# Two-layer streaming encoder on one core: the attention's value products taken per head in two passes

## What is computed

```python
def sb_attend(q, k, v, q_pos, k_pos):
    z = jnp.einsum('bqhd,bkhd->bhqk', q, k).astype(jnp.float32) * SB_SCALE
    visible = k_pos[None, :] < q_pos[:, None]
    log_1mb = jnp.where(visible, jax.nn.log_sigmoid(-z), 0.0)
    suffix = lax.cumsum(log_1mb, axis=3, reverse=True) - log_1mb
    a = jnp.where(visible, jnp.exp(jax.nn.log_sigmoid(z) + suffix), 0.0)
    return jnp.einsum('bhqk,bkhd->bqhd', a.astype(v.dtype), v)
```

## Time and profile before

| | us |
|---|---|
| median of three runs | 1851.74 |
| lowest and highest | 1851.21, 1851.76 |
| the profiled execution's own time | 1851.8 |
| its span in the profile | 1850.0 |
| PE busy in that span | 1829.1 |
| mean granted clock | 1.00 |

### The profile page before, as it was taken

One profiled execution on the slowest core, in us unless ns is written; L12 is line 12 of the kernel. 1 busy time (PEld: TensorE's weight loads), 2 busy tenths in 40 slices (PEclk: granted clock), 3 DMA queues, 4 the chain that ended last, 5 costly groups with the idle time before them and its releaser, 6 DMA issues.

```text
span 1850.0 us, 33796 instructions
## 1 busy us (share of the span) xinstructions
PE 1829.1 (99%) x14262; PEld 1773.7 (96%) x14262; DVE 927.8 (50%) x1634; ACT 559.8 (30%) x1197; POOL 1074.3 (58%) x996
## 2 busy tenths in 40 slices
PE   9999999999999999999999999999999999999999
PEld 8999989999999999999999999899999999999999
DVE  6676775232755532523556767752346555235143
ACT  4444443112422211202344444430133222112021
POOL 8685534746555555556666854446456555555564
PEclk9999999999999999999999999999999999999999
DMA  5242112233223222223343421212422222222222
GB/s 188 88 136 73 63 41 81 92 118 115 70 91 92 83 89 92 86 80 97 98 143 93 127 86 47 69 62 88 152 80 75 86 92 89 84 92 92 80 83 95
DMA packets 76231, 170.49 MB, mean 92 GB/s; under 512 B 6384, under 2 KB 34160, under 8 KB 76080
## 3 DMA queue, kind: packets, MB, share of 16 engines
q1 hardware_dynamic: 68752, 160.79, 27.2%
q10 hardware_dynamic: 7328, 7.54, 1.2%
HBM read 156.41 MB, written 9.79 MB: 90 GB/s over the span
## 4 chain that ended last, share of the span: by engine, by line
PE 92%; DVE 5%; ACT 1%; issue 0%; POOL 0%; DMA 0%; SPq 0%; DVEq 0%; ACTq 0%; POOLq 0%
PE ps L1563 76%; PE ps L1598 2%; PE ps L1726 2%; PE ps L1684 2%; DVE xT L1430 1%; DVE xn L1091 1%; DVE mix L1427 1%; PE ps L1775 1%; PE ps L1781 1%; PE ps L1637 1%; PE ps L1703 1%; DVE R L1091 1%; DVE xT L1248 1%; PE ps L1652 1%; PE ps L1749 1%; PE ps L1722 1%
## 5 line engine op out<-in xcount | busy, mean ns | idle before, releaser
L1563 PE MATMUL ps<-xn,wsp 128*128 128x272 f32 x7824 | 1002.4, 289 | 4.2 <-issue 2.2
L1563 PEld LDWEIGHTS ps<-xn,wsp 128*128 128x128 f32 x7824 | 985.4, 189 | 8.2 <-issue 4.1
L612 POOL CAST wsp<-raw 128x1024 fp32r<-128x1024 f32 (+2 forms) x222 | 219.0, 991 | 505.9 <-DMA raw<-in_wstream 452.1
L619 POOL TENSOR_TENSOR wsp<-raw,wsp 128x1024 fp32r<-128x1024 f32 (+2 forms) x278 | 492.3, 1782 | 16.2
L1563 PE MATMUL ps<-R,wsp 128*128 128x272 f32 x3840 | 486.2, 288 | 0.1
L1563 PEld LDWEIGHTS ps<-R,wsp 128*128 128x128 f32 x3840 | 482.7, 189 | 1.2 <-DVE xT L1120 0.5
L606 POOL TENSOR_TENSOR wsp<-raw,wsp 128x256 fp32r<-128x256 f32 x304 | 240.3, 811 | 12.2
L601 POOL CAST wsp<-raw 128x512 fp32r<-128x512 f32 x152 | 106.3, 699 | 151.8 <-DMA raw<-in_wstream 116.1
L1091 DVE SCALAR_TENSOR_TENSOR R<-ps,R 64x256 fp32r<-64x256 f32 (+11 forms) x264 | 129.8, 510 | 72.2 <-ACT R L749 24.9
L1446 DVE TENSOR_TENSOR mix<-ps,rstd 128x272 f32<-128x272 f32 x88 | 38.8, 441 | 202.5 <-PE ps L1563 192.2
L976 ACT ACTIVATE mix<-vv 128x2 f32<-128x2 f32 x88 | 18.0, 204 | 363.0 <-DVE mix L1448 363.0
(11 more groups left out here) (230 smaller groups left out, 1543.0 us busy)
## 6 DMA issues: line engine op xcount, KB each, us to landing
raw<-in_wstream SPq DMA_DIRECT2D x233, 512.0 KB, 3.5
raw<-in_wstream SPq DMA_DIRECT2D x48, 128.0 KB, 2.7
raw<-in_wstream SPq DMA_DIRECT2D x16, 384.0 KB, 3.1
raw<-in_kc SPq DMA_DIRECT2D x8, 512.0 KB, 3.8
raw<-in_vc SPq DMA_DIRECT2D x8, 512.0 KB, 4.4
xT<-in_x_in SPq DMA_DIRECT2D x8, 272.0 KB, 5.0
out_k_out<-mix ACTq DMA_DIRECT2D x8, 272.0 KB, 2.9
xT<-in_x_in SPq DMA_DIRECT2D x1, 2176.0 KB, 9.3
```

Source lines behind the costliest of these rows:

```text
L612: ins = nc.gpsimd.tensor_copy(dst[:, 0, f], part[:, f])
L619: ins = nc.gpsimd.tensor_tensor(dst[:, 1, f], part[:, f], dst[:, 0, f].bitcast(F32), ALU.subtract)
L1563: mm = pe.matmul(z[:, h], w[:, x, (k0 + k) * P:(k0 + k + 1) * P], rhs[:, y, k, h * HT:(h + 1) * HT], start=(k == 0 and (x, y) == (0, 0)), ...
```

## The change

The value products are taken per head. The stationary operand is now the high part and the low part of one head's values side by side (64 and 64 columns), so that the 128 rows of the result are values-high by weights and values-low by weights. The moving operand is the weights' high part and then their low part, for all four query blocks at once: for key block kb the matmul has (4-kb) times 128 columns, so 512, 384, 256 and 128, two of each, 8 matmuls a head and 16 a pair. There are four products now (low by low too) where there were three. For the second head the query blocks lie in reverse order in the weights' buffer (`at_view`, `at_keys`, `turned`), so that every read is one contiguous run. Both products (`pv0` for the first head, `pv1` for the second) come five steps after the pair's first unit. An evacuation is one ACT copy of 64 partitions by 512 elements, one DVE subtraction of the same size and one DVE addition that adds the lower 64 partitions of the PSUM bank, with a semaphore (`pv_low`) between the two.

`midst`: where the unit before is a sample unit (steps 9 and 18) `pv1` comes behind the first quarter of the step's projections. `sooner`: in the step behind the first latent sample unit (step 35) both evacuations come before the maxima on DVE and before exponents on ACT. In the other latent steps ACT does the exponents of unit s ahead of the high part of unit s-1 and evacuates `pv1` behind both, and DVE evacuates `pv1` behind the normalising. `FILL` changes in steps 3, 5, 8, 12 and 14, and tile `ot` of the first sample unit moves from step 14 to step 12. The weights' buffer is free for the next pair's first unit only behind `pv1`.

```diff
-        at = reg(b1, 2, 2, ATW)
+        at = reg(b1, 2, 2 * ATW)
...
-        v_s = reg(b2, 2, 2, QB, P)
+        v_s = reg(b2, 2, 2 * QB, 2, 64)
...
-            o = qb * (qb + 1) // 2 * P
-            return at[:, x, :, o:o + P * (qb + 1)]
+            a = at[:, x, qb * P:(qb + 1) * P]
+            return bass.AP(tensor=a.tensor, offset=a.offset,
+                           ap=[a.ap[0], [(2 * ATW // P - 1 - 5 * qb) * P, 2], [3 * P, qb + 1], [1, P]])
+
+        def at_keys(x, r, kb):
+
+            o = (2 * ATW // P - 4 - 3 * kb if r else 4 * kb) * P
+            return at[:, x, o:o + (QB - kb) * P]
+
+        def turned(ap, r):
+
+            z = ap.rearrange("p (b q) -> p b q", q=P)
+            return z[:, ::-1] if r else z
...
-                      [4, 4, 4, 3, 3, 3, 4, 4, 3, 4, 4, 4, 3, 2, 3, 2, 3, 3] +
+                      [4, 4, 4, 4, 3, 1, 4, 4, 4, 4, 4, 4, 4, 2, 2, 2, 3, 3] +
                       [2, 2, 1, 2, 1, 2, 2, 2, 1, 1, 2, 2, 1, 1, 2, 2, 2, 4, 0])
-        AFTER = {0: [("vt", 0)], 1: [("ct", 0)], 2: [("vt", 1)], 6: [("vt", 2)], 11: [("vt", 3)], 13: [("ukt", 0)], 14: [("ot", 0)],
+        AFTER = {0: [("vt", 0)], 1: [("ct", 0)], 2: [("vt", 1)], 6: [("vt", 2)], 11: [("vt", 3)], 13: [("ukt", 0)], 12: [("ot", 0)],
                  15: [("kv", 0)], 20: [("kv", 1)], 21: [("ot", 1)], 22: [("ql", 0)], 24: [("kv", 2)], 26: [("ql", 1)],
                  28: [("kv", 3)], 30: [("ql", 2)], 32: [("ql", 3)]}
-        AHEAD = {start(br, t) + d: [("pv" + h + br, t)] for br in "sm" for t in range(PAIRS) for h, d in (("a", 3), ("b", 5))}
+        AHEAD = {start(br, t) + 5: [("pv0" + br, t)] for br in "sm" for t in range(PAIRS)}
+        SECOND = {s: [("pv1" + n[3], t)] for s, ((n, t),) in AHEAD.items()}
...
+        def midst(s):
+            return second(s) if s <= NS and sample(s - 1) else []
+
+        def sooner(s):
+            return s > NS and sample(s - 1)
...
+            whole(*(second(s) if not midst(s) else []))
...
-            some(fills(s))
+            some(fills(s)[:1])
+            whole(*midst(s))
+            some(fills(s)[1:])
...
-                        if t[0] == "pvas" and t[1] == 2:
-                            act.wait_ge(pre["qr_in"], QR_MOVES * (layer + 1))
-                        o, q = (o_sb if t[0][3] == "s" else o_ml), slice(0, SEQ // 2) if t[0][2] == "a" else slice(SEQ // 2, SEQ)
-                        for r in range(2):
-                            ins = ac(o[64 * r:64 * r + 64, 0, t[1], q], bank(t)[64 * r:64 * r + 64, 256 * r:256 * r + 256], ACT.Copy)
-                        ins.then_inc(S["act_read"], 1)
+                        z = turned(bank(t)[0:64], r)
+                        o = (o_sb if t[0][3] == "s" else o_ml)[64 * r:64 * r + 64, 0, t[1], 0:SEQ]
+                        ac(turned(o, 0), z, ACT.Copy).then_inc(S["act_read"], 1)
...
-                        elif t > 0 and qb in (0, 2):
-                            act.wait_ge(S["p_done"], AT[(("pva" if qb == 0 else "pvb") + br, t - 1)] + 1)
+                        elif t > 0 and qb == 0:
+                            act.wait_ge(S["p_done"], AT[("pv1" + br, t - 1)] + 1)
...
+                        if s == NS:
+                            nc.scalar.preload_act_table_set("natural_log_exp_and_others")
+                        for t in second(s) if sooner(s) else []:
+                            evacuate(t, s)
+                        if NS <= s < NU and second(s):
+                            exponents(s)
                         if s > 0:
                             weights_hi(s - 1)
-                        if s == NS:
-                            nc.scalar.preload_act_table_set("natural_log_exp_and_others")
-                        if NS <= s < NU:
+                        if NS <= s < NU and not second(s):
                             exponents(s)
-                        for t in after(s) + [t for t, i in fills(s) if i == 3]:
+                        for t in (second(s) if not sooner(s) else []) + after(s) + [t for t, i in fills(s) if i == 3]:
...
-                        o, q = (o_sb if t[0][3] == "s" else o_ml), slice(0, SEQ // 2) if t[0][2] == "a" else slice(SEQ // 2, SEQ)
-                        for r in range(2):
-                            lo(o[64 * r:64 * r + 64, 1, t[1], q], bank(t)[64 * r:64 * r + 64, 256 * r:256 * r + 256],
-                               o[64 * r:64 * r + 64, 0, t[1], q], "dve_read" if r else None)
+                        r, z = int(t[0][2]), bank(t)
+                        o = (o_sb if t[0][3] == "s" else o_ml)[64 * r:64 * r + 64, :, t[1], 0:SEQ]
+                        lo(turned(o[:, 1], 0), turned(z[0:64], r), turned(o[:, 0], 0), "pv_low")
+                        dve.wait_ge(S["pv_low"], PV_AT[t] + 1)
+                        v.tensor_tensor(turned(o[:, 1], 0), turned(z[64:128], r), turned(o[:, 1], 0).bitcast(F32),
+                                        ALU.add).then_inc(S["dve_read"], 1)
 
...
-                        elif s < NU:
+                        elif s < NU and not sooner(s):
                             maxima(s)
-                        for t in ahead(s):
+                        for t in ahead(s) + (second(s) if sooner(s) else []):
                             evacuate(t)
+                        if s < NU and sooner(s):
+                            maxima(s)
                         if s > 0:
                             weights_lo(s - 1)
                         if s < NS:
-                            for t in after(s):
+                            for t in (second(s) if not midst(s) else []) + after(s):
                                 evacuate(t)
                             products(s)
                         elif s < NU:
                             normalise(s)
-                        for t in (after(s) if s >= NS else []) + [t for t, i in fills(s) if i == 3]:
+                        for t in ((second(s) if not sooner(s) else []) + after(s) if s >= NS else midst(s)) + [t for t, i in fills(s) if i == 3]:
...
+                                j = qb - kb if r else kb
+                                mm = pe.transpose(ps[:, ZB + 2 * (n % 2) + r, j * P:(j + 1) * P], x[:, r, kb * P:(kb + 1) * P], ident)
...
-                        br, p = t[0][3], t[1]
-                        n = start(br, p) + (1 if t[0][2] == "a" else 3)
-                        val, o = (v_s if br == "s" else vm)[:, p % 2], 0 if t[0][2] == "a" else 3 * P
+                        br, p, r = t[0][3], t[1], int(t[0][2])
+                        val = (v_s if br == "s" else vm)[:, p % 2]
                         banks_free(t)
-                        if t[0][2] == "a":
+                        if r == 0:
                             pe.wait_ge(S["dve_read"], dread(("vt" if br == "s" else "kv", p)))
-                        pe.wait_ge(S["at_lo"], n + 1)
-                        z, blocks = bank(t).rearrange("p (r q) -> p r q", r=2), 2 if t[0][2] == "a" else QB
-                        for kb in range(blocks):
-                            for i, (x, y) in enumerate(PARTS):
-                                if kb == blocks - 1:
-                                    mm = pe.matmul(z[:, :, P:2 * P], val[:, x, kb], at[:, y, :, o + 2 * kb * P:o + (2 * kb + 1) * P],
-                                                   start=False, stop=(i == 2))
-                                else:
-                                    a = at[:, y, :, o:o + 2 * (blocks - 1) * P].rearrange("p r (b q) -> p r b q", b=2)
-                                    mm = pe.matmul(z.rearrange("p r (b q) -> p r b q", b=2), val[:, x, kb],
-                                                   a[:, :, :, kb * P:(kb + 1) * P], start=(kb == 0 and i == 0), stop=False)
+                            pe.wait_ge(S["at_lo"], start(br, p) + QB)
+                        for kb in range(QB):
+                            w = (QB - kb) * P
+                            z = bank(t)[:, 0:w] if r else bank(t)[:, 512 - w:512]
+                            for x in range(2):
+                                mm = pe.matmul(z, val[:, 2 * kb + r].rearrange("p x f -> p (x f)"), at_keys(x, r, kb),
+                                               start=(kb == 0 and x == 0), stop=(kb == QB - 1 and x == 1))
...
+                        for t in second(s) if not midst(s) else []:
+                            pv(t)
...
-                        quarters(fills(s))
+                        quarters(fills(s)[:1])
+                        for t in midst(s):
+                            pv(t)
+                        quarters(fills(s)[1:])
```

More of the change, by code:

```diff
@@ L183, in build @@
         q_smp = reg(b3 + 2 * PAIRS * P, 2, PAIRS, P)
-        vm = reg(b3, 2, 2, QB, P)
+        vm = reg(b3, 2, 2 * QB, 2, 64)
         ol_s = reg(b3, 2, 2 * P)
@@ L241, in z_view, with z_blocks @@
             return ps[:, ZB + 2 * (n % 2):ZB + 2 * (n % 2) + 2, 0:w]
+        def z_blocks(n, qb):
+            return z_view(n, P * (qb + 1)).rearrange("p r (b q) -> p r b q", q=P)
         def bt_view(n, w):
```

(45 more changed lines are left out.)

9 lines of the change are left out of this document (4 added, 5 removed).

## The result

The changed kernel takes 1865.45 us (median of 6 runs, 1863.73 to 1866.49) against 1851.74 before (1851.21 to 1852.23): ratio 1.0074, 95% interval 1.0063 to 1.0084. It is slower by 13.7 us where 5.6 us of gain were forecast, and it lies outside the range. The profiled execution took 1866.49 us, the highest of the six and 1.0 over their median; its span is 1864.6.

The account below looks back on a forecast made before the run. PE's work was taken as the bound. Per layer: -7.9 us work, -2.7 old waits, +8.2 new waits less 0.4, so -2.8, or -5.6 in all from 1851.8: 1846.2 us, range 1838.5 to 1851.

Parts of the forecast that it names:

- What PE's work is worth: Value products on PE: a pair falls from 3.68 to 2.64 us, 15.8 us saved in all, 7.9 a layer.
- The rival of slow operations: DVE's evacuation operations take 0.94 us, not 0.68: 7.3 us more, 1853.5 us, slower than before; chance 0.08.
- the rival by which the products stay at 3.6 us a pair: Narrow matmuls don't pipeline, so PE's products save nothing and only waits differ: about 1857 us; chance 0.02.
- transposes of unit 5: PE comes 3.0 us earlier and waits for DVE's four operations: a new wait of 1.2 us.
- step 12: Projection qn0 still waits for the evacuation of k3, whose banks it takes: 1.1 us of saved work not gained.
- scores of step 19: Wait for unit 17's high and low parts, held until pv1 has read the buffer in step 18: 1.1 us.
- kv(3) and ql(3): Steps 28 and 32: tiles wait for both banks, pv1's evacuation being behind normalising: 1.0 us each, 2.0 together.
- gb3: Projection in step 35 waits for its banks' evacuation: 1.2 us where it was about 0.9, 0.3 more.
- step 36: Unit 35's weights come late, as evacuation, maxima, exponents and normalising run serially: a new wait of 1.6 us.
- the last sentence on step 18: It claimed that three quarters in step 9 cover the wait that costs 1.1 us in step 18.
- The term of step 5: Two quarters leave the step: new waits of 1.2 us at unit 5's transposes and 0.6 around it, 1.8.
- the old waits that go: Waits at steps 28 and 32 and around 3 to 4 and 12 to 13 disappear: 2.7 us a layer.

Follow-up runs that it names:

- e3: Changed kernel with two edits: rotation of qr(1) behind the evacuation of pv0s(1) in step 9, one quarter moved from step 3 back to step 5; 1845.55 us.
- e1: Changed kernel, in step 9 alone DVE takes the rotation of qr(1) behind the evacuation of pv0s(1), not ahead of the scans; 1854.34 us.
- e7: On top of e3: in step 35 DVE takes the maxima of unit 35 ahead of the evacuations again; 1842.44 us.
- e10: On top of e7: DVE's addition in each evacuation left out, so the low values' contribution is missing; 1835.55 us.
- e2: Changed kernel with one quarter moved from step 3 back to step 5, so that qr(0) ends in step 4; 1857.82 us.
- e4: Changed kernel with DVE's addition in each evacuation left out, so the low values' contribution is missing; 1851.46 us.
- e5: Changed kernel with three projection quarters, not one, ahead of pv1s(1) in step 9, and both ahead of pv1s(3) in step 18; 1861.54 us.
- e8: On top of e3: kv(3) moved from step 28 to 29 and ql(3) from step 32 to 33; 1849.98 us.

## Why the prediction was wrong

**What PE's work is worth: right.** Forecast -7.9 us a layer. e3's window has 260.07 us busy against 267.94, -7.87. A pair takes 2.58 (82.82 to 85.40 in the changed kernel, 80.91 to 83.49 in e3) where 2.64 was forecast. The starts within e3's pair are 231, 175, 119 ns apart for 512, 384, 256 columns, as taken. Of two matmuls of 128 columns the next start comes 61 to 63 ns behind the first and 111 behind the second, where 110 was taken for both; that makes 0.1 us a pair. The Trainium skill, "TensorE: Matmul & The Clock Gate", section "Back-to-back issue gap", has 56 ns for an isolated one of 128 columns: the first of the two is near it, the second is not. (The forecast's 15.2 us without the extras is 15.0 by its own prices: 16 times 3.48 less 2.54.)

**DVE's operations: right.** Forecast 0.68 each, measured 0.678 and 0.694. The rival of slow operations is dead, its sign (slower than before) came true for another reason. So is the rival by which the products stay at 3.6 us a pair; its 1857 was also too low, since with the sum's own waits, 5.1 a layer, it comes to some 1861. Slower had a chance of 0.05 in the forecast.

**The waits: most near, two wrong.** In layer 0: transposes of unit 5, forecast 1.2, measured 1.15, but behind two other waits, and 0.71 in e3, where they are gone; step 12, 1.1 against 1.05; scores of step 19, 1.1 against 1.03; kv(3) and ql(3), 2.0 against 1.3; gb3, 0.3 more against 0.56 more (1.37 against 0.81); step 36, 1.6 against 1.34; step 8, 0.3 against nothing.

**The step that failed** is the last sentence on step 18, by which step 9 was put at nothing: "In step 9 three quarters cover the same." I took step 9 as step 18 with more cover, and looked at what follows `pv1s(1)`, not at what it waits for. The quarters stand behind `pv1s(1)`; only one stands ahead. Both steps make `pv1` wait for the bank of `pv0`, but in step 18 DVE is at once free for that evacuation, and in step 9 it has 4.1 us of rotation and 1.7 of scans in its queue first. Forecast 0, measured 3.5 to 3.7 us of waiting and 1.6 to 2.9 more by the clock: 6.5 us in layer 0 and 5.3 in layer 1 (the jump from ztS0 to v3 against e3's), 11.8 in all. e1 takes most of it away by moving that rotation alone.

**The term of step 5 was mis-sized** for the same cause. I costed the two quarters that leave step 5 and not that one of those added in step 3 completes qr(0), by which its rotation goes past the scans of step 4 and the low part of unit 3. Forecast 1.8 us around step 5; in e3, where the quarter is back, it is 0.71 there, and 0.45 and 0.36 in step 4, where the forecast had a gain. Against e3 the changed kernel loses 3.8 and 5.1 us more up to ztS0, the clock included: 8.9 in all. The rotation that came along with the quarter was left out of the count.

**The clock was not priced at all.** It is 4.4 us of layer 0's stage and 4.2 of layer 1's (PE busy in each against e3), both already in the two amounts above. It isn't a third cause: in e3 both waits are gone and the clock stays up in both stages.

**The rest of the sum holds, in part by luck.** With both mistakes taken out of the kernel, the stage has 8.9 us of idle time a layer (269.0 - 260.07), within the 7 to 10 forecast, and the time is 1845.55 against 1846.2. But two errors cancel in that. In layer 0 the old waits that go are some 1.9 us, not 2.7, and the new ones 6.8, not 7.8 (8.2 less 0.4). 11.8 and 8.9 make 20.7 us, against 20.4 between the two spans. The 1.34 us of step 36 are a loss of the reorder by itself, as e7 shows; the prediction took it as the price of an earlier evacuation, and none was bought.

Not tried: a bank of its own for `pv1s(1)`, which would need v3 or the emptying of ztS0's bank moved as well, and the addition on another engine, for which e10 gives the bound, 6.9 us.

## What to carry to other kernels

When a piece of work is moved to an earlier step, write down the whole queue of every engine that empties its output, with the long instructions that come along, before costing the cover. A tile that must wait for a bank filled one moment earlier depends on the order of the emptying engine's queue, not on that engine's load: here DVE was idle for nearly a third of the stage. And an idle stretch can cost more than its length, since the work behind it may run at the lower clock: here 1.7 and 2.7 us on top of 3.5.

## What was unexpected of the hardware

The same wait doesn't bring the clock down each time, nor for the same time. Behind the wait of e2 in step 9, 3.52 us in both layers, it was low for 3.4 us in layer 0 and 6.8 in layer 1. In e4 that wait is 2.79 us in both layers: the clock was low for 6.8 us in layer 0 and never fell in layer 1. As all else is alike there, this prices the fall once more: from ztS0 to v3 layer 0 takes 2.8 us longer. The wait of 2.58 us in e5 left it up in layer 0 and brought it down for 3.4 us in layer 1.

Shorter waits are as uneven. Waits of 1.3 to 1.4 us (gb3, and in e3 another 7.6 us later) left it up, and one of 1.29 in e8 was followed by a fall, in some executions and not in others. Outside the stages, a wait of 1.75 us at 885.59 in the changed kernel was followed by 3.4 us at the lower level, where the same wait in the kernel before, 1.76 us at 877.98, was not. The waits of 1.47, 1.64 and 1.15 within 9 us in the changed kernel brought it down in both layers; with 1.48, 0.80 and 0.43 at the same place, in e4, it stayed up. So the length of a wait alone doesn't decide; what does isn't shown here.

Of two equal matmuls of 128 columns in a row behind wider ones, the next start comes 61 to 63 ns behind the first and 111 behind the second.
